# Two stacked transformer blocks on one core: embedding product ahead of its gates, one pass for two norms, output projection by k-tiles

## The reference

```python
# first block
h = rmsnorm(x, norm_mix_g); proj = h @ w_in                  # attention, recurrence, latent attention, gates
merged = sum(sigmoid(gate_logits) * (branch @ w_branch))     # three branches
x = x + merged @ w_out
x = x + square(relu(rmsnorm(x, norm_ffn_g) @ w_ff1)) @ w_ff2
x = rmsnorm(x, final_norm_g)                                 # the norm between the blocks
# second block, for i in 0, 1
h = x
u = rms_norm(h, attn_norm_w[i]); proj = u @ w_in[i]
fox = forgetting_attention(...)                              # 8 heads, 512 features
ret = silu(rg) * head_group_norm(chunkwise_retention(...))   # 8 heads, 512 features
h = h + concatenate([fox, ret]) @ w_out[i]
h = h + gated_conv_ffn(rms_norm(h, ffn_norm_w[i]), ...)
gate = sigmoid(rms_norm(h, ple_norm_w[i]) @ w_ple_gate[i])   # 1024 x 1024
h = h + gate * (p[i] @ w_ple_proj[i])                        # p[i]: 512 x 256, the embedding
# at the end
return rms_norm(h, final_norm_w)
```

## Time and profile before

| | |
|---|---|
| time, median of 3 runs | 2589.27 us (2587.88 to 2592.51) |
| the profiled execution's own time | 2589.27 us |
| its span in the trace | 2587.2 us |
| TensorE busy | 2414.7 us, 93% |
| GpSimd busy | 1172.7 us, 45% |
| VectorE busy | 1111.4 us, 43% |
| ScalarE busy | 892.8 us, 35% |
| mean granted TensorE clock | 0.969 of full speed |

### The profile page before, as it was taken

The page is one execution under the profiler, slowest core; times in us unless marked ns, Lnnn a source line. Parts: engine busy times, 40 slices in busy tenths (PEclk is TensorE's granted clock), DMA queues, the critical chain, the costliest instruction groups (busy, mean ns, idle before and its releaser), DMA issues.

```text
span 2587.2 us, 37533 instructions
## 1 busy us (share of the span) xinstructions
PE 2414.7 (93%) x11548; PEld 1898.8 (73%) x11548; DVE 1111.4 (43%) x1869; ACT 892.8 (35%) x1364; POOL 1172.7 (45%) x1570
## 2 busy tenths in 40 slices
PE   7998895999999999799989999997999889999996
PEld 5776673767788888577667888886777667888874
DVE  2466566443322223425554434342345544343443
ACT  3354342444322222324324322244323234322253
POOL 5344552225455455433225655555533135645553
PEclk9999997999999999899989999999999999999998
DMA  4221111114232222221112323232211113323222
GB/s 142 82 81 50 45 53 32 49 49 126 94 113 90 89 97 98 71 87 57 65 49 98 106 89 105 84 97 82 88 60 65 65 53 102 106 89 105 85 86 82
DMA packets 62809, 211.14 MB, mean 82 GB/s; under 512 B 7008, under 2 KB 7392, under 8 KB 62736
## 3 DMA queue, kind: packets, MB, share of 16 engines
q1 hardware_dynamic: 56160, 194.27, 22.9%
q10 hardware_dynamic: 6576, 15.97, 1.9%
HBM read 208.05 MB, written 2.16 MB: 81 GB/s over the span
## 4 chain that ended last, share of the span: by engine, by line
issue 49%; POOL 35%; PE 12%; DVE 2%; POOLq 1%; DVEq 1%; ACT 0%; ACTq 0%
POOL w_lo L1591 35%; PE acc L256 4%; PE acc L258 3%; PE acc L257 3%; POOLq L1620 1%; PE po L484 0%; PE sc L383 0%; PE po L333 0%; PE pt L317 0%; DVE cums L1178 0%; PE sc L484 0%; POOLq L1597 0%; POOLq L1588 0%; DVE probs L1028 0%; DVEq L1185 0%
## 5 line engine op out<-in xcount | busy, mean ns | idle before, releaser
L1591 POOL TENSOR_TENSOR w_lo<-raw,w_hi 128x256 fp32r<-128x256 f32 x1506 | 1131.8, 785 | 1332.1 <-ACT w_hi L637 1329.9
L256 PE MATMUL acc<-act_hi,w_hi 128*128 128x512 f32 x2000 | 819.6, 410 | 47.7 <-DVE act_lo L1025 35.9
L258 PE MATMUL acc<-act_hi,w_lo 128*128 128x512 f32 x2000 | 789.4, 395 | 0.0
L257 PE MATMUL acc<-act_lo,w_hi 128*128 128x512 f32 x2000 | 788.5, 394 | 0.0
L637 ACT CAST w_hi<-raw 128x1024 fp32r<-128x1024 f32 (+1 forms) x390 | 393.9, 1020 | 361.7 <-PE acc L258 187.9
L256 PEld LDWEIGHTS acc<-act_hi,w_hi 128*128 128x128 f32 x2000 | 381.0, 190 | 157.7 <-issue 41.6
L258 PEld LDWEIGHTS acc<-act_hi,w_lo 128*128 128x128 f32 x2000 | 380.7, 190 | 82.6
L257 PEld LDWEIGHTS acc<-act_lo,w_hi 128*128 128x128 f32 x2000 | 382.4, 191 | 71.6 <-issue 2.2
L256 PE MATMUL acc<-y_hi,w_hi 128*128 128x512 f32 x880 | 354.1, 402 | 27.7 <-DVE y_lo L1045 12.2
L258 PE MATMUL acc<-y_hi,w_lo 128*128 128x512 f32 x880 | 347.4, 395 | 0.0
L257 PE MATMUL acc<-y_lo,w_hi 128*128 128x512 f32 x880 | 347.3, 395 | 0.0
(11 more groups left out here) (271 smaller groups left out, 2132.7 us busy)
## 6 DMA issues: line engine op xcount, KB each, us to landing
raw<-in_w_ffn_wide SPq DMA_DIRECT2D x120, 512.0 KB, 3.3
raw<-in_w_in SPq DMA_DIRECT2D x104, 512.0 KB, 3.3
raw<-in_w_rest SPq DMA_DIRECT2D x72, 512.0 KB, 3.3
raw<-in_w_gate SPq DMA_DIRECT2D x24, 512.0 KB, 3.3
raw<-in_w_ple_gate SPq DMA_DIRECT2D x16, 512.0 KB, 3.3
raw<-in_w_branch SPq DMA_DIRECT2D x24, 256.0 KB, 2.6
raw<-in_w_ffn_narrow SPq DMA_DIRECT2D x16, 384.0 KB, 3.0
x<-in_x ACTq DMA_DIRECT2D x16, 256.0 KB, 3.4
```

What stands on the lines that cost most here:

```text
L256: nc.tensor.matmul(dst, w[0], src[0], start=start, stop=False)
L257: nc.tensor.matmul(dst, w[0], src[1], start=False, stop=False)
L258: return nc.tensor.matmul(dst, w[1], src[0], start=False, stop=stop)
L1591: last = nc.gpsimd.tensor_tensor(w_lo[:, slot, cut], raw[:, slot % 2, cut], w_hi[:, slot, cut], ALU.subtract)
```

## The change

1. **First two panels.** `normed_gemm` now begins with `first_two`: k-tiles 0 to 6 of two panels, then the wait for the last activation tile, then k-tile 7 of both, and only then the sum over partitions. It is used at all places with a norm ahead of a product, now also in the first feed-forward of block one and at the entry to layer 0 and 1.
2. **One pass between the blocks.** The pass r = 2 adds up the squares of x and those of x times the gain, makes the tiles for layer 0 from the unscaled x with the product of both gains, and `mid_factor` derives both factors from one pass. DVE still scales x (8 instructions), now between two multiplications for the factors.
3. **Output projection by k-tiles.** `fox_half` runs k-tiles 0 to 3 of four panels between the matmuls of the group norm; then each of k-tiles 4 to 7 over the same four panels; then the other four panels as before. ACT casts two panels ahead of the group norm's squares, the other six in the loop of `norm_tile`.
4. **Embedding first.** The 3 embedding panels come ahead of the gate's 8. ACT copies their eight tiles from PSUM to `wa`. Then each gate panel j is scaled by DVE, passed through Sigmoid by ACT, multiplied and added into x by DVE, and goes through `norm_tile` for the next norm.
5. **End.** The last norm's tiles are x times the final gain, made by ACT; five are multiplied by the factor on DVE and three on POOL, and stored in the order 0, 5, 1, 2, 6, 3, 4, 7.
6. The loops over the two layers are written out; the embedding's split is moved behind feed-forward chunk 0; layer 1 takes its activation tiles from `y_hi`, `y_lo` (tiles 4 to 11).

```diff
-            def normed_gemm(layer, first, count, r, split):
-                gemm(layer, first, 1, KD, act_in, (S("norm_split"), split * 8))
+            def first_two(layer, first, r, src, base):
+                for j in range(2):
+                    pe.wait_ge(lo_done, layer + (first + j + 3))
+                    pe.wait_ge(acc_free, layer + (first + j + 1))
+                    tile_products(acc[:, (first + j) % 4, :], (first + j) % 4, 0, P, KD, src, base,
+                                  None if j else (S("norm_split"), r * 8), range(KD - 1))
+                pe.wait_ge(S("norm_split"), r * 8 + KD)
+                for j in range(2):
+                    tile_products(acc[:, (first + j) % 4, :], (first + j) % 4, 0, P, KD, src, base, None,
+                                  range(KD - 1, KD)).then_inc(gemm_done, 1)
+
+            def normed_gemm(layer, first, count, r, src=act_in, base=0):
+                first_two(layer, first, r, src, base)
                 norm(r)
-                gemm(layer, first + 1, count - 1, KD, act_in)
+                gemm(layer, first + 2, count - 2, KD, src, base=base)
...
                 for p in range(PAIRS):
-                    head_mean("r_o", l * 4 + (p + 1), "r_mean", p, wa[:, p, :])
+                    head_mean("r_o", l * 4 + (p + 1), "r_mean", p, wa[:, p, :], ret_bank)
+                fox_half(0)
                 for p in range(PAIRS):
-                    head_mean("r_sq", l * 4 + (p + 1), "r_var", p, wb[:, p, :])
-                gemm(layer, N_BLOCK1 + O_O, 8, KD, y_in, (S("r_y"), l * 4, 4))
+                    head_mean("r_sq", l * 4 + (p + 1), "r_var", p, wb[:, p, :], ret_bank)
+                    if p < 3:
+                        fox_half(p + 1)
+                for k in range(4, KD):
+                    pe.wait_ge(S("r_y"), l * 4 + (k - 3))
+                    for j in range(4):
+                        slot = (O_O + j) % 4
+                        last = tile_products(acc[:, slot, :], slot, 0, P, KD, y_in, part=range(k, k + 1))
+                        if k == KD - 1:
+                            last.then_inc(gemm_done, 1)
+                gemm(layer, N_BLOCK1 + O_O + 4, 4, KD, y_in)
...
-                normed_gemm(layer, N_BLOCK1 + O_GATE, 8, l * 3 + 5, l * 3 + 4)
                 pe.wait_ge(S("e_split"), l * 2 + 2)
+                for m in range(KD):
+                    q, bank = m // 3, (O_PLE + m) % 4
...
+                    if m < 4:
+                        pe.wait_ge(acc_free, layer + (N_BLOCK1 + O_PLE + m + 1))
+                    else:
+                        pe.wait_ge(S("e_free"), l * 8 + (m - 3))
+                    last = tile_products(acc[:, bank, :], slot, (m % 3) * 2 * P, P, 2, y_in, 8)
+                    last.then_inc(gemm_done if m in (2, 5, 7) else S("e_done"), 1)
+                pe.wait_ge(S("e_free"), l * 8 + 8)
+                normed_gemm(layer, N_BLOCK1 + O_GATE, 8, l * 3 + 4)
```

On ACT:

```diff
+            def mid_factor():
+                act.wait_ge(S("norm_sum"), 3)
+                factor(mid_rstd, sc[:, 0, :], 1.0 / D, "eps").then_inc(S("mid_rstd"), 1)
+                act.wait_ge(S("mid_square"), 1)
+                factor(rstd[:, :], mid_square, 1.0 / D, "eps").then_inc(S("mid_factor"), 1)
...
+                for j in range(2):
+                    high(half, full, N_BLOCK1 + O_O + LOOK + j)
                 for p in range(PAIRS):
                     act.wait_ge(S("r_d"), l * 4 + (p + 1))
                     nc.scalar.activation(wb[:, p, :], wa[:, p, :], ACT.Square).then_inc(S("r_sq"), 1)
...
-                split_ahead(half, full, N_BLOCK1 + O_O, 8,
-                            lambda k, odd: norm_tile(l * 3 + 4, k, odd, l * 3 + 3, "ffn_w", l * KD))
-                norm_factor(l * 3 + 4)
+                for j in range(KD):
+                    if j > 1:
+                        high(half, full, N_BLOCK1 + O_O + LOOK + j)
+                    norm_tile(l * 3 + 3, j, j % 2, "ffn_w", l * KD)
+                norm_factor(l * 3 + 3)
...
+                for m in range(KD):
+                    if m % 3 == 0:
+                        high(half, full, N_BLOCK1 + O_PLE + LOOK + m // 3)
...
+                    nc.scalar.copy(wa[:, m, :], acc[:, (O_PLE + m) % 4, :]).then_inc(S("e_free"), 1)
+                act.drain().then_inc(acc_free, 3)
+                norm_factor(l * 3 + 4)
+                for j in range(KD):
+                    high(half, full, N_BLOCK1 + O_GATE + LOOK + j)
+                    in_place(ACT.Sigmoid, "e_g", "e_gate", l * 8 + j, wb[:, j, :])
+                    if j == KD - 1:
+                        ln_exp_table()
+                    if l + 1 < LAYERS:
+                        norm_tile(l * 3 + 5, j, j % 2, "attn_w", l * KD + KD, attn_tiles(l + 1))
+                    else:
+                        norm_tile(l * 3 + 5, j, j % 2, "final_g", 0, (wb, None, 0))
                 norm_factor(l * 3 + 5)
```

On DVE, in each layer and at the end (and on POOL):

```diff
+                for j in range(KD):
+                    n, slot = layer + (N_BLOCK1 + O_GATE + j), (O_GATE + j) % 4
+                    gate = wb[:, j, :]
+                    guest(n, slot, gate, "e_g")
+                    dve.wait_ge(S("e_gate"), l * 8 + (j + 1))
+                    settle(dve)
+                    v.tensor_tensor(gate, gate, wa[:, j, :], ALU.mult)
                     dve.drain()
+                    v.tensor_tensor(x[:, j, :], x[:, j, :], gate, ALU.add)
+                    dve.drain().then_inc(S("norm_x"), 1)
+                    if l + 1 < LAYERS:
+                        norm_tile(l * 3 + 5, j, j % 2, "attn_w", l * KD + KD, attn_tiles(l + 1))
+                    else:
+                        norm_tile(l * 3 + 5, j, j % 2, None)
+                norm_end()
+            dve.wait_ge(S("norm_rstd"), 9)
+            for k in range(5):
+                v.tensor_tensor(wb[:, k, :], wb[:, k, :], rstd[:, :], ALU.mult).then_inc(S("out_ready"), 1)
...
+            pool.wait_ge(S("norm_rstd"), 9)
+            for k in range(5, KD):
+                nc.gpsimd.tensor_tensor(wb[:, k, :], wb[:, k, :], rstd[:, :], ALU.mult).then_inc(S("out_ready_too"), 1)
```

More of the change, by code:

```diff
@@ L606, in _ @@
                     if ch == 0:
[L607 removed]
+                        normed_gemm(layer, first, 2 * tiles, l * 3 + 3)
                     else:
@@ L728, in _ @@
             act.wait_ge(S("param_loaded"), 16)
-            norm(0, 0, "mix_g")
+            for k in range(KD):
+                norm_tile(0, k, k % 2, "mix_g")
+            norm_factor(0)
             act.wait_ge(S("const_loaded"), 32)
```

221 lines of the change are left out of this document (113 added, 108 removed).

## The result

The changed kernel takes 2604.39 us in the median of four runs (2603.12 to 2605.43), the kernel before 2588.57 us beside it (2587.78 to 2592.51): ratio 1.0054, 95% interval 1.0042 to 1.0066, 15.8 us slower. The forecast was 2595.9: the sign was right, the measured time lies inside the range of 2581 to 2608, and 8.5 us were missing. The profiled execution took 2603.92 us, its span is 2601.4 us (14.2 more than before), and the mean granted clock is 0.964 instead of 0.969.

A forecast was written before the change was run, and what follows sets the result against it. TensorE, busy 93% of the span, was taken as the bound, so only its waits could change. Terms 6.3 + 1.8 - 7.5 + 0 + 10.9 - 3.7 - 1.2 = +6.6 us on 2589.27 gave 2595.9 us, range 2581 to 2608.

The forecast's parts named there:

- chain W: At every norm: sum to third panel takes at least 6.4 us, now exposed, so PE idles about 5.4 us.
- C: Between the blocks: 31.4 us to layer 0's third panel becomes 22.3, with the half clock 23.9: -7.5 us.
- F: Gate and embedding of layer 0, up to layer 1's third panel: gate tiles 6.2 us apart, -3.7 us with the clock.
- A: Start of the program: the third panel starts 4.7 us later, +6.3 us with the half clock.
- B: First feed-forward, block one: 17.1 us to the third panel becomes 17.3, +0.2 us, with the half clock +1.8.
- E: Output projection to feed-forward, twice: the second panel hides nothing, +5.4 us each, +10.9 together (9 to 14).
- D: Output projection, twice: a 10 us gain given back, as PE idles 8.1 us at the fifth panel: 0 (-2 to +3).
- Rival 1: Output projection: the fifth panel does not wait for ACT, so the kernel ends faster, 2576.5 us; chance 0.12.
- G: Gate of layer 1 to the end: 86.6 us becomes 85.0 plus 0.4 for contention: -1.2 us (-6 to +3).
- Rival 2: Gate loop: the DVE and ACT ping-pong fits in a panel, pitch 5.4 us, no change, 2588 us; chance 0.18.
- Rival 4: Gate loop: Square needs another table than Sigmoid, two loads a tile, 37 us more, 2633 us; chance 0.03.
- Rival 3: Exposed chains cost more, by slower POOL subtractions or half clock lasting twice as long: about +10 us, 2606; chance 0.15.

The follow-up runs named there:

- the fill: Kernel after the change with 22 more matmuls behind each sum over the partitions, keeping TensorE busy while it would wait for the third panel's weights: 2594.96 us.

## Why the prediction came out as it did

**The chain W** was right in kind and size: 6.28 at the gate and 6.35 at the entry to layer 1 (1831.82 to 1838.17) for the forecast's 6.4, and 7.22 in block one. The waits for `w_lo` grew by 62.7 us where the forecast had some 50; its list left out those at the entries to the layers, 10.34 and 5.34, which its terms C and F had counted. The kernel with one panel takes 44.7 us off, and the kernel before with two is 48.8 us slower; both directions show that the first part of the change is the loss.

**A, B, E**, without the clock, measured +5.6, +1.0 and +10.7 for +4.7, +0.2 and +10.9. Of A's 0.9 too much, 0.74 is a later start (first matmul at 13.85 for 13.11). B's 0.8 too much is the chain, 7.22 for 6.4: POOL's subtractions there took 0.92 us each for 0.785. E came as argued: before, PE did not wait ahead of the sum there, and the second panel had nothing to hide.

**C** measured -8.35 for -9.1. The forecast had DVE's scalings off PE's path but for 0.5 us (at most 1) that they cost POOL. Beside them POOL took 1.85 longer: from the start of the subtraction to the panel are 4.76 us (1067.41 to 1072.17), against 2.91 in the earlier trace rows; the other terms were 0.6 too large together. POOL in block one and between the blocks, two panels each:

```profile
706.57 7.33 POOL L1672 TENSOR_TENSOR w_lo<-raw,w_hi 128x256 fp32r<-128x256 f32 x8 [13.38 <-ACT w_hi L681]
...
1067.41 7.82 POOL L1672 TENSOR_TENSOR w_lo<-raw,w_hi 128x256 fp32r<-128x256 f32 x8 [16.54 <-ACT w_hi L681]
```

**D** measured -0.2 for 0, its two places together, with a wait of 7.52 for the forecast's 8.1. That the cast's place makes the loss is shown: moved, it gives 5.1 us a layer back. That the gain against it is of the same size follows from the wait and the sum; no run shows it alone. Rival 1 is out; the fifth panel waited over 5 us.

**F and G** measured -4.3 and -1.6 for -5.3 and -1.2. F's 1.0 too much is there at the sum of layer 1's entry, which came 80.5 us after F's start (1831.82) for the forecast's 79.4. In layer 0 the pitch was 6.23 (1800.61 to 1806.84) for 6.2. Its make-up was off: multiply and add took 1.28 and 1.05 beside POOL, not 0.69 each, so the handovers were shorter than I had them, and that the sum of the parts came out is luck. G is luck in part too: the pitch in layer 1 was 5.55 for 5.9 (POOL at 2549.77, 2555.32, 2560.87), some 2 us sooner at the last sum, and the last products and stores took 9.5 for 7.8. Rival 2, a pitch near 5.4, is out in layer 0 and nearly holds in layer 1, where the slow end took its gain. That the cast's place paces PE too was right and of no weight: the cast one further ahead took PE's wait and not the loop's pace.

**Rival 4** is out: between 1801.90 and 1804.14 ACT goes from the square (L722) by a cast to the Sigmoid (L769) without a table load.

**The sum** was 7.6 us short in the span, and no one step failed. The steps are 2.7 of it, most of that in A, B, C and F. The stretches are 4.9, and all of it is the clock. Those right behind a long wait were later by 1.3 (first scores of block one, 89.07 to 96.01), 1.4, 1.3, 1.1, 2.3 and 0.7, together 8.1 us where the half clock had 6.4. Here the term was mis-sized at the layers' feed-forwards, which I gave none, since a spell stood there already: it grew to 10.2 us, 5.8 of them under full work. The 9.4 us that the fill gave back can't be held against the 6.4: they are what part of the half clock costs in the kernel after, and the forecast's term is what is new against the kernel before. The other 3.2 are +4.8 in the two stretches to the head means less 1.6 in block one. They are half clock at other places of the same work, which the forecast had no term for; whether the change has a part in where it falls stays open, and profiles of one kernel repeated would be needed.

**Rival 3** gave 2606 and came nearest in number, but not by its mechanism as a whole. Its first half, slower subtractions in each exposed chain, holds at some of them only: from POOL's start to the panel are 3.72 us in block one, 3.80 at layer 0's feed-forward (where the whole chain is as long as before, 8.68 for 8.70) and 4.76 between the blocks, but 2.91 at the start and 2.82 at layer 0's gate, for 2.91 in the earlier trace rows. The half clock of its second half is 1.7 us over the 6.4, not double.

## What to carry to other kernels

Before work is put ahead of a reduction, look at both its sides: it hides a wait in front only if there is one, and it uncovers the whole chain behind (factor, cast, subtraction, next panel) where that was covered. In-order engines make the chain: whether the next panel's cast stands ahead of or behind the factor was worth 35 us with two panels ahead of the sum, and 9 in the kernel before with one. A wait that vanishes without the time moving, as at the gate's fourth panel, says that another engine paces the stretch, and then the thing to bring forward is its start. The fastest kernels here keep the change's other parts, one panel ahead of the sum (two at the entry to layer 1) and all casts early: 2.0 to 2.4% faster than the kernel before.

## What the runs showed of the hardware

VectorE's instructions with two SBUF inputs can slow down a good deal while GpSimd works. In the gate's loop of layer 0 the first multiply and add have POOL idle beside them and took 0.69 us each; the seven behind them took 1.26 to 1.28 and 1.05 to 1.07. Five products beside GpSimd took 6.30 us, eight alone 4.90. GpSimd's three tiles took 1.70 us each there (5.10 for three). From the products to the end are 9.5 us with three of the eight on GpSimd and 8.0 without. It is not so for every such pair: in layer 1 the same multiply beside the same subtraction took 0.72 (the add 1.05 to 1.07 again), and there POOL's four took 3.73 instead of 3.26. The first multiply of layer 0, one of layer 1, and POOL's subtractions beside it:

```profile
1780.92 0.69 DVE L1648 TENSOR_TENSOR wb<-wb,wa 128x512 f32<-128x512 f32 x1 [2.23 <-ACT wb L769]
...
2556.59 0.72 DVE L1648 TENSOR_TENSOR wb<-wb,wa 128x512 f32<-128x512 f32 x1 [0.96 <-ACT wb L769]
...
2555.32 3.73 POOL L1672 TENSOR_TENSOR w_lo<-raw,w_hi 128x256 fp32r<-128x256 f32 x4 [1.82 <-ACT w_hi L681]
```

The GPSIMD Engine Reference of the Trainium skill (Specifications) says that GpSimd's SBUF interfaces are shared with VectorE, with contention when VectorE's instruction has two SBUF inputs. That the slow rows stand beside GpSimd's work agrees.

TensorE's clock, 0.50 behind a wait of 7.66 us, stayed there for 5.8 us of work; with other matmuls in most of that wait it was 3.0 us. Behind two waits of 3.08 us ahead of the same matmuls it was 1.00 in one kernel and 0.50 in the other. The same instructions took between 179.0 and 183.0 us in one stretch of layer 0, and between 181.0 and 185.3 in that of layer 1, from kernel to kernel. So a difference under some 5 us in one pair of profiles is not read as an effect of an edit, unless the rows at the edit show it.
